# Recurrent layer of a two-block network: the input product regrouped, its bracket and two low weight parts given to GpSimd

## The reference

```
gate, xr = split(x @ w_in)                       # 1024 columns each
xr = causal_depthwise_conv(xr, conv_w, conv_b)   # 4 taps
r = sigmoid(block_diag(xr, gate_a)); i = sigmoid(block_diag(xr, gate_x))
log_a = -8 * r * softplus(-a_param)
a = exp(log_a)
u = sqrt(-expm1(2 * log_a)) * (i * xr)
h = scan over time: h_t = a_t * h_(t-1) + u_t
y = (h * gelu(gate)) @ w_out
```

## Time and profile before

| | us |
|---|---|
| median of 3 runs | 2967.16 |
| profiled execution, its own time | 2966.62 |
| span of its core in the trace | 2964.7 |
| PE busy | 2930.5 (99% of the span) |
| DVE busy | 1644.9 (55%) |
| ACT busy | 1149.5 (39%) |
| POOL busy | 146.5 (5%) |
| mean granted TensorE clock | 0.998 |

### The profile page before, as it was taken

The page is one execution under the profiler, slowest core; times in us unless marked ns, Lnnn a source line. Parts: engine busy times, 40 slices in busy tenths (PEclk is TensorE's granted clock), DMA queues, the critical chain, the costliest instruction groups (busy, mean ns, idle before and its releaser), DMA issues. The chain is left out here.

```text
span 2964.7 us, 37569 instructions
## 1 busy us (share of the span) xinstructions
PE 2930.5 (99%) x14365; PEld 2440.7 (82%) x14365; DVE 1644.9 (55%) x2337; ACT 1149.5 (39%) x1592; POOL 146.5 (5%) x297
## 2 busy tenths in 40 slices
PE   8999999999999999999999999999999999999999
PEld 7888888888888888868888888768888888888887
DVE  7747476444653336875433357756535567754453
ACT  4223253222432225464332234554423338443242
POOL 0101001000010001040000000110000001000000
PEclk9999999999999999999999999999999999999999
DMA  7837326544362222241322223422322322323222
GB/s 296 275 127 261 122 78 225 173 165 148 121 220 93 99 99 98 89 171 68 114 93 99 99 72 100 145 87 86 106 93 93 101 90 80 106 85 107 93 99 72
DMA packets 100914, 366.56 MB, mean 124 GB/s; under 512 B 11248, under 2 KB 11808, under 8 KB 100784
## 3 DMA queue, kind: packets, MB, share of 16 engines
q1 hardware_dynamic: 77616, 276.56, 27.6%
q0 software_dynamic: 23168, 88.17, 8.8%
HBM read 362.51 MB, written 2.18 MB: 123 GB/s over the span
## 5 line engine op out<-in xcount | busy, mean ns | idle before, releaser
L1027 DVE TENSOR_TENSOR wl<-raw,wh 128x1024 fp32r<-128x1024 f32 x501 | 609.6, 1226 | 967.2 <-ACT wh L549 966.8
L549 ACT ACTIVATE wh<-raw 128x1024 fp32r<-128x1024 f32 x501 | 524.2, 1055 | 1195.3 <-PE PS L1763 1146.4
L1763 PE MATMUL PS<-HH,wh 128*128 128x512 f32 x2432 | 947.0, 389 | 6.0 <-DVE HL L1611 3.9
L1763 PE MATMUL PS<-HL,wh 128*128 128x512 f32 x2432 | 946.2, 389 | 0.0
L1763 PE MATMUL PS<-HH,wl 128*128 128x512 f32 x2432 | 946.1, 389 | 0.0
L1763 PEld LDWEIGHTS PS<-HH,wh 128*128 128x128 f32 x2432 | 456.5, 188 | 103.3 <-DVE HL L1611 5.2
L1763 PEld LDWEIGHTS PS<-HH,wl 128*128 128x128 f32 x2432 | 456.5, 188 | 95.2
L1763 PEld LDWEIGHTS PS<-HL,wh 128*128 128x128 f32 x2432 | 456.5, 188 | 93.9
L1763 PE MATMUL PS<-AH,wh 128*128 128x512 f32 x848 | 330.1, 389 | 0.5 <-DVEq L1646 0.5
L1763 PE MATMUL PS<-AH,wl 128*128 128x512 f32 x848 | 329.9, 389 | 0.0
L1763 PE MATMUL PS<-AL,wh 128*128 128x512 f32 x848 | 329.9, 389 | 0.0
(11 more groups left out here) (279 smaller groups left out, 3138.0 us busy)
## 6 DMA issues: line engine op xcount, KB each, us to landing
raw<-in_stream SPq DMA_DIRECT2D x501, 512.0 KB, 3.3
acc<-in_stream POOLq DMA_DIRECT2D x86, 512.0 KB, 4.8
piece<-in_stream POOLq DMA_DIRECT2D x42, 512.0 KB, 4.8
arena<-in_stream SPq DMA_DIRECT2D x16, 512.0 KB, 12.5
TBa<-negcum POOLq DMA_DIRECT2D x8, 640.0 KB, 4.9
TBa<-in_alibi POOLq DMA_DIRECT2D x8, 640.0 KB, 4.7
TBb<-negcum POOLq DMA_DIRECT2D x4, 640.0 KB, 4.5
piece<-negcum POOLq DMA_DIRECT2D x4, 640.0 KB, 6.0
```

The source lines that it names most:

```text
L549: F(wh[:, r, :], raw[:, r, :], ACT.Copy).then_inc(hi_done, 1)
L1027: TT(wl[:, r, :], raw[:, r, :], wh[:, r, :].bitcast(F32), ALU.subtract).then_inc(lo_done, 1)
L1763: mm = MM(PS[g % 2][:, j, :], l, x, start=(first and i == 0), stop=(last and i == 2), skip_group_check=after_halves)
```

## The change

For t >= 4 the product (e+1)*root*(i*x) is grouped another way. Before, DVE made (e+1)*root (L1665) and multiplied with i*x (L1670). Now POOL makes the bracket (e+1)*(i*x) as e*(i*x) + (i*x), in two instructions, and DVE multiplies once with the root (`decayed_input`). POOL also makes the four products i*x for t >= 4, and the low parts of the chunks `cd+2` and `cd+3`. POOL's new instructions are 12 of 128x512 (four times L541, L547 and L548) and 2 of 128x1024 (L553). DVE loses four of L1676, four of L1665 and two of L1027. In the last four tiles `y_lo(t-1)` now stands between the product and the scan, and DVE waits for POOL's two chunks before it goes on with `cd+4`.

```diff
@@ gpsimd
                         pl.tensor_tensor(lru_i(t), lru_i(t), lru_x, ALU.mult).then_inc(ix_done, 1)
+                    pl.wait_ge(ix_done, 8)
+                    for t0 in (4, 6):
+                        for t in (t0, t0 + 1):
+                            pl.wait_ge(gates_done, 2 * t + 2)
+                            pl.wait_ge(rc_conv, t + 1)
+                            pl.tensor_tensor(lru_i(t), lru_i(t), WK[:, t % 4, :], ALU.mult).then_inc(ix_late, 1)
+                        for t in (t0, t0 + 1):
+                            pl.wait_ge(exp_done, t + 1)
+                            pl.wait_ge(ix_late, t0 - 2)
+                            if t > 4:
+                                pl.wait_ge(ix_scaled, t - 4)
+                            pool_link(pl.tensor_tensor(lru_x, lru_r(t), lru_i(t), ALU.mult))
+                            pl.tensor_tensor(lru_i(t), lru_x, lru_i(t), ALU.add).then_inc(ix_scaled, 1)
+                    for c in (st["c"] + 20, st["c"] + 21):
+                        r = c % RING
+                        pl.wait_ge(hi_done, c + 1)
+                        pl.wait_ge(lo_done, c)
+                        pl.tensor_tensor(wl[:, r, :], raw[:, r, :], wh[:, r, :].bitcast(F32), ALU.subtract).then_inc(lo_done, 1)
@@ vector
                     def scan(t):
-                        dve.wait_ge(*((ix_done, 2 * t + 2) if t < 4 else (ix_late, t - 3)))
-                        link(TT(lru_r(t), lru_r(t), lru_i(t), ALU.mult))
+                        if t < 4:
+                            dve.wait_ge(ix_done, 2 * t + 2)
+                            link(TT(lru_r(t), lru_r(t), lru_i(t), ALU.mult))
                         nc.vector.tensor_tensor_scan(lru_i(t), lru_a(t), lru_r(t), 0.0, ALU.mult, ALU.add).then_inc(y_done, 1)
-                    def gated_input(t):
-                        dve.wait_ge(gates_done, 2 * t + 2)
-                        TT(lru_i(t), lru_i(t), WK[:, t % 4, :], ALU.mult).then_inc(ix_late, 1)
+                    def decayed_input(t):
+                        dve.wait_ge(root_done, t + 1)
+                        dve.wait_ge(ix_scaled, t - 3)
+                        link(TT(lru_r(t), lru_t(t), lru_i(t), ALU.mult))
...
                     split_until(cb + 3)
-                    gated_input(4)
-                    gated_input(5)
...
                     y_lo(1)
-                    gated_input(6)
-                    gated_input(7)
                     split_until(cd + 1)
...
                     split_until(cd + 2)
                     for t in range(4, KT):
-                        factor(t)
-                        scan(t)
+                        decayed_input(t)
                         if t > 4:
                             y_lo(t - 1)
+                        scan(t)
                         gated_output(t)
-                        if t < 6:
-                            split_until(cd + t - 1)
                     y_lo(KT - 1)
+                    dve.wait_ge(lo_done, cd + RING)
+                    at["split"] = cd + RING
```

More of the change, by code:

```diff
@@ L365, in build @@
             "gate_used", "gates_done", "tanh_done", "exp_done", "t_read", "root_done"))
-        ix_late = sem("ix_late")
+        ix_late, ix_scaled = sem("ix_late"), sem("ix_scaled")
         ix_done, y_done, gelu_ready, y_prod, y_hi = (sem(n) for n in (
```

## The result

The changed kernel takes 2975.38 us (median of 10 runs, 2974.48 to 2976.01) against 2966.90 us of the kernel before (median of 10, 2965.60 to 2967.36): +8.5 us, a ratio of 1.0029 with a 95% interval of 1.0021 to 1.0038. Slower, as forecast (2975.6).

What follows compares the result with a forecast made beforehand. DVE's chain was taken to set PE's waits around the projection. Its second half 7.8 us later plus 0.7 for the clock gave +8.5 on 2966.62, 2975.1, and 0.5 for the median made 2975.6; range 2971.0 to 2978.5.

Steps and rivals of the forecast that it cites:

- DVE's chain sets the stretch: From 2500 to `y_lo(7)`, PE follows DVE's chain; 5.2 us is all there is to gain.
- What goes from DVE: Work removed from DVE: 1.2 us ahead of the projection's start, 5.2 behind it; the first two `gated_input` gain nothing.
- A turn costs DVE 1.03 for ten instructions: Ahead of the projection, each of POOL's ten 128x512 instructions holds DVE up for 1.03 us, 10.3 in all.
- The low part of `cd` at 2522.8, PE idle for some 9 us: At the projection's start, DVE's low part of `cd` ends 9.1 us later and PE idles, where it idled 0.2.
- POOL's 128x1024 at 2.43, holding DVE for 2.2; 3.2 for both: Behind the projection's start, two POOL instructions on tile 5's product and scan cost DVE about 1.0 and 2.2 us.
- 1.2 for `y_lo(4)` behind gelu and two weight copies: `y_lo(4)`, now ahead of scan 5, waits for its high half on ACT, costing about 1.2 us.
- The second half 7.8 later, 0 to 1.1 more by the clock: The projection's second half starts at 2548.2 to 2548.3 instead of 2540.50; a slow PE clock may add 1.1 us.
- the clock's 0.7: Amount taken for PE's clock falling to near half after the idle stretch ahead of the projection, between nothing and 1.1 us.
- The range: Likeliest case 2972.3 to 2978.5, from bounds of about +5.3 and +11.6 us; stated range 2971.0 to 2978.5.
- What would show it: Trace signs: POOL's 128x512 at 1.7 to 2.4 us after 2500, DVE's 1.8 for 0.69, PE idle 8 to 9 ahead of projection.
- The rival that POOL runs at no cost: POOL runs beside DVE without disturbing it, so only the removals count: -5.0 us, 2962.2; chance 0.10.
- The rival that POOL starves: DVE keeps the port while it has work and POOL runs only when DVE waits: +4.2 us, 2971.4; chance 0.06.

Runs made afterwards that it cites:

- the run with four brackets: Kernel before, nothing added on POOL, with DVE making the brackets (e+1)*(i*x) of tiles 0 to 3 in its idle time: 2966.75 us against 2966.62.
- the spare products: Kernel before plus ten POOL instructions of 128x512 that nobody waits for: 2973.80 us as in-place subtractions (against 2966.72), 2976.06 as products of two ranges (against 2966.32).
- the fills: Kernel before plus three POOL memsets of a spare 128x512 tile in each of ten places, reading nothing from SBUF: 2966.77 us against 2966.72.
- the kernel with low parts only: Kernel before with only the low parts of `cd+2` and `cd+3` moved to POOL, two instructions of 128x1024: 2968.74 us against 2966.72.
- the filled kernel: Changed kernel with 34 matmuls on the identity in PE's idle time ahead of the projection, to keep the clock up: 2975.54 us against 2966.62 before the change.
- the kernel with all brackets early: Kernel before with DVE making the brackets of tiles 0 to 3 in idle time and of 4 to 7 in two later gaps: 2964.28 us against 2966.32.

## Why the prediction was right, step by step

- **DVE's chain sets the stretch, and a microsecond added ahead of the low part of `cd` is one of PE's.** Right for time that is added: the low part of `cd` came 8.8 us later (9.06 in the trace, 0.3 of which the execution brought along), PE waited 8.4 more there, and the run took 8.5 longer. Not right for time that is taken away: ACT is as late as DVE, and relieving DVE by 2.9 ahead of that place gave nothing.
- **What goes from DVE.** The first two `gated_input` free, as in the trace. The 1.2 of the other two would not have been a gain by itself, by the run with four brackets; it counted here only because POOL's turns had made DVE late.
- **A turn costs DVE 1.03 for ten instructions.** Measured 0.99 each. It was the step on which the sign hung, and the spare products show it without any of the change's own waits. By the rule of the Trainium skill (page SBUF — State Buffer, section Who interferes with whom) the other engine is blocked for the whole instruction: the trace has DVE lose 0.81 to 1.10 of POOL's 1.30, so the rule is right in kind, and DVE lost a quarter less than it says. That it is the read side which DVE needs, which the same section of the Trainium skill says, the fills bear out: thirty of them left the time as it was.
- **The low part of `cd` at 2522.8, PE idle for some 9 us.** 2522.72 and 8.43. The first is so close by luck: the ten turns cost 0.4 less than forecast, and the execution was 0.3 late.
- **POOL's 128x1024 at 2.43, holding DVE for 2.2; 3.2 for both.** They took 2.40 and 2.66. Where DVE was busy one cost it 2.19, and 2.2 and 2.0 in the kernel with low parts only; 0.77 + 2.19 = 3.0 for both in the changed kernel. They fell on `y_lo(4)` and the scan of tile 5, where the forecast had that tile's product and scan.
- **1.2 for `y_lo(4)` behind gelu and two weight copies.** DVE stood 1.45 there; putting the scan first gave at most 0.9 back.
- **The second half 7.8 later, 0 to 1.1 more by the clock.** 8.7 later in the trace, 0.3 of which it brought along: 8.4, where the forecast had 8.5. That the sum came so close is luck: it was off in three places that cancel. The turns cost 0.4 less. The chain behind the projection's start was longer: 2545.58 + 0.69 = 2546.27 less 2522.72 is 23.6, not 22.6. Of that 1.0 the trace shows nearly 0.4 where DVE's product waits for its own scan after POOL's turn (0.46, usually 0.1), 0.3 in two waits for ACT's high parts, and 0.25 in the longer wait for `y_lo(4)`; the rest is open. And the clock's 0.7 should have been 0. The clock did fall, and it cost PE 1.9 us up to the end of k = 4, but PE would have waited that long for `y_lo` in any case, as the filled kernel's 2.84 for 1.06 shows. The forecast's own sum for it does not come out either: two slow units end at 2522.9 + 2 x 5.44 + 6 x 2.72 = 2550.1, which is 1.8 more, not 1.1.
- **The range.** Its lower end is not what its terms give: 9.0 + 3.2 - 2.3 - 1.2 is 8.7, not 5.3, and the case that it describes, turns at 0.9 and nothing for the two large ones, would be 7.8 - 1.3 - 3.2 = +3.3. The result lay far from that end.
- **What would show it.** PE's waits ahead of k = 5, 6 and 7 were forecast at 1 to 3 us and measured 1.06, 0.36 and 0.31, since PE came there late itself.
- **The rival that POOL runs at no cost** was out, by the spare products. Whether it was priced rightly no run shows: the kernel with all brackets early relieves DVE behind that place of 2.9 and not of 5.2, and gained 2.0. **The rival that POOL starves** was out: POOL got a turn at each end of a DVE instruction.

## What to carry to other kernels

Before giving elementwise work to GpSimd, look at what DVE does in that stretch. If both work on pairs of SBUF tensors, they take turns: here a turn cost DVE's chain 1.0 where DVE would have done the work itself in 0.60 to 0.72. Where DVE was idle it was free. A regrouping that makes part of a product independent of the late factor can be had on DVE itself, put into its own gaps: that took 2.0 us off here, with an interval that just reaches no change, where the version with GpSimd added 8.5. And before counting on a gain from relieving one engine, ask who is second: here ACT, busy 98% of the same stretch, was as late as DVE.

## What the runs showed of the hardware that I had not expected

A POOL subtraction of a tile from itself, in place, cost DVE only 0.77 per instruction of 128x512, where products of two different ranges cost 1.01 and the changed kernel's mix 0.99. In each case the cost is POOL's own time for the instruction (1.04 and 1.30 at the shortest) less 0.3, and for 128x1024 it is 2.40 less 0.2 to 0.4. And a DVE instruction that is held up looks busy: the changed kernel's DVE shows 5 us more of busy time with less work, and no wait for POOL in its list.
